# Order of the units and of the table loads in the long convolutions of an encoder layer

## The chip, the core and the metric

The kernel runs on one core of one Trainium2 chip. The metric is the device time of one execution in microseconds (us), smaller being better.

The engines are called here as the profile calls them: PE (TensorE, matrix products), PEld (its weight loads), DVE (VectorE), ACT (ScalarE), POOL (GpSimd) and SP (SyncE, which here only starts transfers).

## What is computed

One encoder layer for two sequences, of 528 and 272 tokens with their 16 meta tokens (below: the long and the short sequence): a windowed attention and a Hyena long convolution side by side, gated and merged, then a mixture of experts. The change touches only the long convolutions:

```
def _long_conv(z, kf):
    L = z.shape[1]
    zf = jnp.fft.rfft(z, n=2 * L, axis=1)
    return jnp.fft.irfft(zf * kf[None], n=2 * L, axis=1)[:, :L]

def _hyena(u, conv_w, conv_b, kf, skip):
...
    v, x1, x2 = jnp.split(uc, HY_ORDER + 1, axis=-1)
    z = v.astype(F32)
    sk = skip.astype(F32)
    for o, gate in enumerate((x1, x2)):
        z = gate.astype(F32) * (_long_conv(z, kf[:, o]) + sk[o] * z)
    return z.astype(u.dtype)
```

`kf` is the spectrum of a filter that the kernel makes itself. The 512 channels are four tiles of 128.

## The kernel before

Three stages follow one another: `stage_mix` (projections, attention, the short convolution), `stage_hyena` (the long convolutions) and the block of `stage_route` and `stage_experts`. At the end of each of the first two stands a barrier of all engines.

`stage_hyena` has eight **units**, one for each sequence and channel tile. `UNITS` (line 935) lists them as (sequence, tile): sequence 0 is the long one, 1 the short one. Each unit is gone through twice, once for each order of the recurrence `o`. Such a pass is a **turn**, and `TURNS` (line 936) fixes the 16 of them: turns 0 to 3 are `o` = 0 of units 0 to 3, turns 4 to 7 are `o` = 1 of the same units, and turns 8 to 15 are the same for units 4 to 7. A turn whose unit is long is called a long turn.

The Fourier transforms are matrix products with tables: `ahead` (to the spectrum) and `back` (from it), one set for each length, each with a small `_rest` table for the last rows. Values are split in a high and a low part, and a product is three PE passes (lines 250 to 252) over them. The steps of a turn:

- `hgen` (PE, lines 1266 and 1267): filter taps from the features and the output weights, three tiles. It needs both halves of the weights of its channel tile `j`, with the wait `pe.wait_ge(w_lo, j + 1)`. These halves are made once per channel tile by `wsum` (POOL, lines 315 and 316), `whi` (ACT, lines 1369 and 1370) and `wlo` (DVE, line 1459).
- `decay` (DVE, line 1483): taps times a decay table that SP loads (three buffers); for a long turn `hsum` (POOL, lines 1115 and 1116) adds and subtracts them; `hhi` (ACT, lines 1383 to 1388) and `hlo` (DVE, lines 1492 and 1494) split them.
- `kf` (PE, lines 250 to 252 and 1282) makes the filter's spectrum with `ahead`. It needs all three `hlo` of its turn. A long turn has two `kf` steps of 14 products, a short one has one. `kfout` (ACT, lines 1399 and 1400) takes it out of PSUM.
- `fold` (POOL, lines 1130 and 1131, long turns of `o` = 0 only), `zt` (PE transposes, lines 1302 to 1308), `zhi` (ACT, lines 1411 to 1414), `zlo` (DVE, lines 1501 and 1502), `fwd` (PE, again 14 products a step, two steps in a long turn).
- `mul` (DVE, line 1515), `comb` (POOL, lines 1144 and 1145), `yt` (PE transposes, line 1336), `yhi` (ACT), `ylo` (DVE), `inv` (PE, with `back`), `gate` (DVE) and, in long turns, `unfold` (POOL).

`hyena_steps` (line 943) gives each step a place, its turn's number plus the constant of `PLACE` (line 937), and sorts all steps by it. Every engine goes through this one list in its order and takes its own steps. So the steps of neighbouring turns overlap, and an engine that waits holds back whatever stands behind on it. The products go round robin through four pairs of PSUM banks.

The tables of `stage_hyena` are loaded by POOL's queue, from within that list at `wsum` of tile 0 and of tile 1 (lines 1100 to 1107). Tile 0's sums were made in the stage before. Decay tables and rows of the sequences come by SP's queue. In turns 0 to 3 before: short tile 0, long tile 0, long tile 1, short tile 1.

Of the kernel before, what the change touches and what calls it, by code (L numbers as in the profile page):

```python
# [310 lines left out]
def sum_weights(nc, g, j):  # L311

    both = g.wraw[:, :, j * P:(j + 1) * P].rearrange("k (r o) c -> k r o c", r=2)
    dst = g.wsum[:, :, :].rearrange("k (r o) c -> k r o c", r=2)
    nc.gpsimd.tensor_tensor(dst[:, 0, :, :], both[:, 0, :, :], both[:, 1, :, :], ALU.add)
    nc.gpsimd.tensor_tensor(dst[:, 1, :, :], both[:, 0, :, :], both[:, 1, :, :], ALU.subtract).then_inc(g.w_sum, 1)
# [615 lines left out]


WRAW_AT = 217984 + 64
UNITS = [(1, 0), (0, 0), (0, 1), (1, 1), (0, 2), (0, 3), (1, 2), (1, 3)]
TURNS = [(4 * g + k, o) for g in range(2) for o in range(2) for k in range(4)]
PLACE = {"wsum": -3.2, "whi": -3.35, "wlo": -2.65, "hgen": -2.95, "decay": -2.65, "hsum": -2.35, "hhi": -2.25, "hlo": -1.55, "kf": -1.05, "kfout": -0.95,
         "fold": -0.95, "zt": -0.9, "zhi": -0.85, "zlo": -0.5, "fwd": -0.25, "mul": 0.1, "comb": 0.35, "yt": 0.65, "yhi": 0.75, "ylo": 1.05, "inv": 1.5, "gate": 1.75, "unfold": 2.55}
# [4 lines left out]
def hyena_steps():  # L943
# [7 lines left out]
    for i, (u, o) in enumerate(TURNS):  # L951
        s = UNITS[u][0]
        for k in ("hgen", "decay", "hhi", "hlo") + (("hsum",) if s == 0 else ()):
# [10 lines left out]
def stage_hyena(g):  # L964
    nc, io, S = g.nc, g.io, g.sem
# [6 lines left out]
    back = [sb(f"back{s}", [P, 2, BT[s], BN[s]], F32R) for s in range(2)]  # L972
    back_rest = [sb(f"back{s}_rest", [96, PAIRS[s], BN[s]], F32R) for s in range(2)]
# [34 lines left out]
    ahead_in, back_in = S("hy_ahead0 hy_ahead1"), S("hy_back0 hy_back1")  # L1008
# [6 lines left out]
    def length(u):  # L1015
        return UNITS[u][0]
    parts = [PAIRS[length(u)] for u, o in TURNS]
# [4 lines left out]
    place = {i: same[s].index(i) for s in same for i in same[s]}  # L1022
    which = {u: UNITS[u][1] for u in range(len(UNITS))}

# [4 lines left out]
    def earlier(u):  # L1029

        return UNITS.index((length(u), which[u] - 2))

# [51 lines left out]
    with nc.Block() as block:  # L1084
        @block.gpsimd
        def _(pool):
            def table_load(tab, dst, sem):
                nc.gpsimd.dma_start(dst[:, :, :, :], io[tab].rearrange("x (t p) w -> p x t w", p=P)).then_inc(sem, 16)
# [5 lines left out]
            for st in steps:  # L1094
                if st[0] == "wsum":
                    j = st[1]
                    if j:
                        pool.wait_ge(w_lo, j)
                        sum_weights(nc, g, j)
                    if j == 0:  # L1100
                        table_load("ahead0", ahead[0], ahead_in[0])
                        nc.gpsimd.dma_start(ahead_rest[0][:, :], io["ahead0_rest"]).then_inc(ahead_in[0], 16)
                    if j == 1:
                        table_load("back1", back[1], back_in[1])
                        nc.gpsimd.dma_start(back_rest[1][:, 0, :], io["back1_rest"]).then_inc(back_in[1], 16)
                        table_load("back0", back[0], back_in[0])
                        nc.gpsimd.dma_start(back_rest[0][:, :, :], io["back0_rest"].rearrange("b p w -> p b w")).then_inc(back_in[0], 16)
                elif st[0] == "hsum":
# [59 lines left out]
        def _(sp):  # L1168
            rows = g.hyS.rearrange("(q j p) t -> j p q t", q=3, p=P)

            def decay_in(i):
                s, j = UNITS[TURNS[i][0]]
                d = decay[i % 3]
                if i >= 3:
                    sp.wait_ge(decayed, MT * (i - 2))
                c = slice(j * P, (j + 1) * P)
                if s == 0:
                    for r in range(2):
                        sp.dma_start(d[:, r, 0:2, :], io["decay0"][r, 0:2 * P, c].rearrange("(t p) c -> p t c", p=P)).then_inc(dec_in[i % 3], 16)
                    sp.dma_start(d[0:REST[0], :, 2, :], io["decay0"][:, 2 * P:FOLD, c].rearrange("r p c -> p r c")).then_inc(dec_in[i % 3], 16)  # L1180
                else:
                    sp.dma_start(d[:, 0, 0:2, :], io["decay1"][0:2 * P, c].rearrange("(t p) c -> p t c", p=P)).then_inc(dec_in[i % 3], 16)
                    sp.dma_start(d[0:REST[1], 0, 2, :], io["decay1"][2 * P:LENS[1], c]).then_inc(dec_in[i % 3], 16)

            def vx_load(u):
                s, j = UNITS[u]
                at = (0, LENS[0] + 1)[s]
                if j >= 2 and s:
                    sp.wait_ge(gate_mul, turn_of(earlier(u), 0) + 1)
                if j >= 2 and s == 0:  # L1190
                    sp.wait_ge(folded, 2 * folds_before[turn_of(earlier(u), 0)] + 2)
                sp.dma_start(vx[s][j % 2][:, :, 0:LENS[s]], rows[j, :, 0:2, at:at + LENS[s]]).then_inc(vx_in[buf(u)], 16)
# [1330 lines left out]
```

## Time and profile before

| | before |
|---|---|
| Median of 3 runs | 1928.94 us (1928.61 to 1931.06) |
| Profiled execution, span | 1928.8 us |
| PE busy | 1835.1 us (95%) |
| DVE busy | 1417.5 us (73%) |
| ACT busy | 1197.9 us (62%) |
| POOL busy | 312.4 us (16%) |
| Mean granted PE clock | 0.976 of full |

The span runs from the first to the last instruction of one profiled execution. It is 0.1 us from the median of the timed runs; no other time of the profiled execution is given. Busy times are those of the whole span. The long convolutions take its part from about 417 to 609 us. The granted clock is told as a share of full speed, 1.0 being 2.4 GHz and 0.5 being 1.2 GHz.

### The profile page before, as it was taken

Reading aid. Unit: us, or ns where it says so; the run is one execution under the profiler, and the core shown is the slowest. Engines: PE = TensorE matmul, PEld = TensorE weight load, DVE = VectorE, ACT = ScalarE, POOL = GpSimd, SP = SyncE. Lnnn points to the kernel's source line nnn. Section 1 sums busy time; section 2 is a strip of 40 time slices with the busy share of each in tenths; the row PEclk is TensorE's granted clock in tenths of the full one; section 3 lists DMA queues with packets and bytes.
Section 4 is the critical chain, followed back from the end, with each engine's and each line's share of the span. In section 5 each row is a group of like instructions: output and inputs, shape, how many; then the busy total and the mean of one; then the engine's idle time right before and its main releaser. Section 6 shows DMA issues by size and latency. Waiting matters only on the chain.

```text
span 1928.8 us, 25301 instructions
## 1 busy us (share of the span) xinstructions
PE 1835.1 (95%) x9358; PEld 1447.1 (75%) x9358; DVE 1417.5 (73%) x1451; ACT 1197.9 (62%) x1332; POOL 312.4 (16%) x220
## 2 busy tenths in 40 slices
PE   5999999978998999599999999999999999999996
PEld 4989877868998988477777777777777777777774
DVE  4673321138885533699999999999999999999996
ACT  4225666644554311377777777777777777777775
POOL 1223211225653500001001000000000110010010
PEclk8999999988999999799999999999999999999998
DMA  6333222145115662599999999999999999999994
GB/s 188 99 82 102 72 71 77 41 140 162 33 44 177 220 230 109 200 356 357 385 385 373 380 382 379 374 391 371 373 382 387 376 379 379 375 376 390 379 352 175
DMA packets 240329, 506.53 MB, mean 263 GB/s; under 512 B 22017, under 2 KB 56681, under 8 KB 240200
## 3 DMA queue, kind: packets, MB, share of 16 engines
q1 hardware_dynamic: 229640, 484.64, 69.6%
q0 software_dynamic: 10624, 21.03, 4.4%
q8 instruction: 40, 0.66, 0.1%
q14 instruction: 25, 0.20, 0.0%
HBM read 474.64 MB, written 31.28 MB: 262 GB/s over the span
## 4 chain that ended last, share of the span: by engine, by line
PE 65%; DVE 2%; ACT 1%; issue 0%; DMA 0%; POOL 0%; DVEq 0%; POOLq 0%; ACTq 0%
PE bank L251 21%; PE bank L250 21%; PE bank L252 21%; PE bank L2141 2%; PE bank L1938 1%; PE bank L1924 0%; DMA gathered<-ffn_rows,slot_tokens 0%; PE bank L245 0%; DVE top_values L1844 0%; DVE top_index L1846 0%; ACT we_hi L2199 0%; DVE affinity L1847 0%; DVE gated L1785 0%; DVE we_lo L2273 0%; DVE bank L1786 0%
## 5 line engine op out<-in xcount | busy, mean ns | idle before, releaser
L2273 DVE TENSOR_TENSOR we_lo<-w_ring,we_hi 128x2048 fp32r<-128x2048 f32 x382 | 864.9, 2288 | 71.1 <-ACT we_hi L2199 64.9
L2199 ACT ACTIVATE we_hi<-w_ring 128x2048 fp32r<-128x2048 f32 x380 | 724.3, 1914 | 98.1 <-PE bank L252 98.0
L250 PE MATMUL bank<-we_hi,gathered_turned_hi 128*100 128x512 f32 x1024 | 404.3, 395 | 1.5 <-DVE gathered_turned_lo L2277 1.5
L251 PE MATMUL bank<-we_lo,gathered_turned_hi 128*100 128x512 f32 x1024 | 404.3, 395 | 0.0
L252 PE MATMUL bank<-we_hi,gathered_turned_lo 128*100 128x512 f32 x1024 | 401.4, 392 | 0.0
L250 PEld LDWEIGHTS bank<-we_hi,gathered_turned_hi 128*100 128x100 f32 x1024 | 168.7, 165 | 67.8 <-issue 1.7
L252 PEld LDWEIGHTS bank<-we_hi,gathered_turned_lo 128*100 128x100 f32 x1024 | 168.7, 165 | 67.0
L251 PEld LDWEIGHTS bank<-we_lo,gathered_turned_hi 128*100 128x100 f32 x1024 | 168.4, 164 | 64.0
L250 PE MATMUL bank<-normed_hi,w_hi 128*128 128x400 f32 x544 | 197.7, 363 | 10.1 <-ACT u_padded L657 5.1
L250 PE MATMUL bank<-we_hi,hidden_turned_hi 128*100 128x512 f32 x512 | 204.4, 399 | 0.0
L251 PE MATMUL bank<-we_lo,hidden_turned_hi 128*100 128x512 f32 x512 | 202.2, 395 | 0.0
L252 PE MATMUL bank<-we_hi,hidden_turned_lo 128*100 128x512 f32 x512 | 201.7, 394 | 0.0
L251 PE MATMUL bank<-normed_lo,w_hi 128*128 128x400 f32 x544 | 188.5, 347 | 0.0
L252 PE MATMUL bank<-normed_hi,w_lo 128*128 128x400 f32 x544 | 188.0, 346 | 0.0
L2119 POOL DMA_INDIRECT residual_rows<-expert_out,slots_now x15 | 42.1, 2807 | 840.2 <-DVE expert_out L2307 840.2
L250 PEld LDWEIGHTS bank<-normed_hi,w_hi 128*128 128x128 f32 x544 | 103.3, 190 | 31.7 <-issue 18.2
L913 POOL TENSOR_TENSOR w_lo<-w_raw,w_hi 128x2048 fp32r<-128x2048 f32 x17 | 79.1, 4652 | 277.3 <-ACT w_hi L622 277.3
L252 PEld LDWEIGHTS bank<-we_hi,hidden_turned_lo 128*100 128x100 f32 x512 | 84.3, 165 | 34.4
L250 PEld LDWEIGHTS bank<-we_hi,hidden_turned_hi 128*100 128x100 f32 x512 | 84.6, 165 | 31.8
L251 PEld LDWEIGHTS bank<-we_lo,hidden_turned_hi 128*100 128x100 f32 x512 | 84.4, 165 | 31.2
L251 PEld LDWEIGHTS bank<-normed_lo,w_hi 128*128 128x128 f32 x544 | 103.3, 190 | 0.0
L252 PEld LDWEIGHTS bank<-normed_hi,w_lo 128*128 128x128 f32 x544 | 103.2, 190 | 0.1
(318 smaller groups left out, 2586.8 us busy)
## 6 DMA issues: line engine op xcount, KB each, us to landing
w_ring<-in_w_exp_gate SPq DMA_DIRECT2D x64, 2048.0 KB, 14.2
w_ring<-in_w_exp_up SPq DMA_DIRECT2D x64, 2048.0 KB, 13.7
w_ring<-in_w_exp_down SPq DMA_DIRECT2D x64, 2048.0 KB, 15.3
w_raw<-in_w_in SPq DMA_DIRECT2D x68, 256.0 KB, 4.2
gate_rows<-gate_sig SPq DMA_DIRECT2D x16, 400.0 KB, 2.5
sig_pair<-gate_rows SPq DMA_DIRECT2D x8, 800.0 KB, 6.1
hy_conv_rows<-u_conv SPq DMA_DIRECT2D x12, 400.5 KB, 3.3
w_out<-in_w_out SPq DMA_DIRECT2D x8, 512.0 KB, 8.5
```

The costliest lines, as they stand in the source:

```text
L250: nc.tensor.matmul(out, whi, xhi, start=first, stop=False)
L251: nc.tensor.matmul(out, whi, xlo, start=False, stop=False)
L252: return nc.tensor.matmul(out, wlo, xhi, start=False, stop=last)
L913: nc.gpsimd.tensor_tensor(wlo[c % 2][:, :, :], raw[c % 3][:, :, :], whi[c % 2][:, :, :].bitcast(F32), ALU.subtract).then_inc(w_lo, 1)
L1938: last = nc.tensor.matmul(g.ps[6][0:m, 0:E], hT[:, k, 0:m], wrg[:, k, :], start=(k == 0), stop=(k == KT - 1))
L2119: pool.indirect_dma_start(g.accS[:, :], bass.IndirectOffsetOnAxis(ap=cur[0:SLOTS, 0:1], axis=0), ye[0:SLOTS, :], None, compute_op=ALU.add) ...
L2141: last = nc.tensor.transpose(tb[n % 2][:, k * P:k * P + SLOTS], src, ident[0:SLOTS, 0:SLOTS])
L2199: act.activation(whi[(2 * k + half) % 4][:, :], ring[k % RING][:, half * HC:(half + 1) * HC], ACT.Copy).then_inc(w_hi, 1)
L2273: nc.vector.tensor_tensor(wlo[u][:, :], ring[k % RING][:, half * HC:(half + 1) * HC], whi[u][:, :].bitcast(F32), ALU.subtract).then_inc(w_ ...
```

## The change

Two things are put in another order, and nothing is added or left out. In `UNITS` the second short unit (1, 1) goes from the fourth place to the second, so turns 0 to 3 become short tile 0, short tile 1, long tile 0, long tile 1. Turns 4 to 7 follow with it; units 4 to 7 are as they were. And the load of the short `back` tables goes from `wsum` of tile 1 to `wsum` of tile 0, ahead of the long `ahead` tables.

```
-UNITS = [(1, 0), (0, 0), (0, 1), (1, 1), (0, 2), (0, 3), (1, 2), (1, 3)]
+UNITS = [(1, 0), (1, 1), (0, 0), (0, 1), (0, 2), (0, 3), (1, 2), (1, 3)]
...
                     if j == 0:
+                        table_load("back1", back[1], back_in[1])
+                        nc.gpsimd.dma_start(back_rest[1][:, 0, :], io["back1_rest"]).then_inc(back_in[1], 16)
                         table_load("ahead0", ahead[0], ahead_in[0])
                         nc.gpsimd.dma_start(ahead_rest[0][:, :], io["ahead0_rest"]).then_inc(ahead_in[0], 16)
                     if j == 1:
-                        table_load("back1", back[1], back_in[1])
-                        nc.gpsimd.dma_start(back_rest[1][:, 0, :], io["back1_rest"]).then_inc(back_in[1], 16)
                         table_load("back0", back[0], back_in[0])
```

What stands in a row on POOL at the start of `stage_hyena`. The names end in numbers of their tensors: `ahead_94` and `back_98` are the short tables, `ahead_93` and `back_97` the long ones; `wout_sum_diff` is written by `wsum`.

```order
 L1088 DMA ahead_94_3774<-in_ahead 128x4x548
 L1091 DMA ahead_rest_3776<-in_ahead_rest 96x548
+L1088 DMA back_98_3778<-in_back 128x8x272
+L1102 DMA back_rest_3780<-in_back_rest 96x272
 L1088 DMA ahead_93_3773<-in_ahead 128x4x1064
-L1102 DMA ahead_rest_3775<-in_ahead_rest 96x1064
-L315 TENSOR_TENSOR wout_sum_diff_56<-filt_wout_55 64x256
-L316 TENSOR_TENSOR wout_sum_diff_56<-filt_wout_55 64x256
-L1088 DMA back_98_3778<-in_back 128x8x272
-L1105 DMA back_rest_3780<-in_back_rest 96x272
+L1104 DMA ahead_rest_3775<-in_ahead_rest 96x1064
```

Two DMA starts now stand ahead of the first `wsum` (lines 315 and 316) of this stage, which was behind four such starts and is behind six.

On DVE, from the last `hlo` of turn 0 to the first `hlo` of turn 1. `taps_ahead_back` is the target of a long turn's `decay`, `taps_sum_diff` that of a short one's; L1459 is `wlo`.

```order
 L1494 TENSOR_TENSOR taps_rest_3810<-taps_sum_diff_3804,taps_rest_3810 16x256
 L1459 TENSOR_TENSOR wout_lo_3795<-wout_sum_diff_56,wout_hi_twice_3794 64x512
-L1483 TENSOR_TENSOR taps_ahead_back_3800<-bank,decay_3798 128x512
-L1483 TENSOR_TENSOR taps_ahead_back_3801<-bank,decay_3798 128x512
-L1483 TENSOR_TENSOR taps_ahead_back_3800<-bank,decay_3798 9x512
+L1483 TENSOR_TENSOR taps_sum_diff_3805<-bank,decay_3798 128x256
+L1483 TENSOR_TENSOR taps_sum_diff_3802<-bank,decay_3798 128x256
+L1483 TENSOR_TENSOR taps_sum_diff_3803<-bank,decay_3798 16x256
 L1459 TENSOR_TENSOR wout_lo_3795<-wout_sum_diff_56,wout_hi_twice_3794 64x512
-L1483 TENSOR_TENSOR taps_ahead_back_3801<-bank,decay_3799 128x512
-L1492 TENSOR_TENSOR taps_lo_3809<-taps_sum_diff_3805,taps_hi_3808 128x512
+L1483 TENSOR_TENSOR taps_ahead_back_3800<-bank,decay_3799 128x512
```

The kinds of steps keep their order here; those of turn 1 are half as wide, and their result is no longer added and subtracted by POOL.

## Rows read from the trace of the kernel before

**Rows 1.** Stretches: length, busy us of PE, PEld, DVE, ACT, POOL, PE clock, DMA share, GB/s.

```profile
421.20:428.10 6.90, 6.16 (x26) 5.03 (x27) 5.89 (x15) 2.81 (x6) 4.91 (x7) 0.52 1.16 369
430.90:437.40 6.50, 0.85 (x7) 0.38 (x5) 3.28 (x6) 4.69 (x11) 4.14 (x6) 0.79 1.21 334
437.40:448.60 11.20, 8.83 (x39) 8.37 (x40) 11.14 (x7) 3.25 (x7) 11.13 (x16) 0.51 1.39 342
452.70:594.00 141.30, 141.30 (x1153) 138.84 (x1152) 114.31 (x197) 73.71 (x178) 73.71 (x100) 1.00 0.15 45
```

**Rows 2.** Who PE waited for from 414 to 612 us: total, times, longest.

```profile
PE bank L250 <- DVE z_turned_rest L1502: 2.9, 1, 2.9
PE bank L250 <- DVE taps_rest L1494: 2.8, 2, 2.4
PE bank L1266 <- ACT spectra L1400: 2.8, 1, 2.8
```

**Rows 3.** PE in order of time: start us, us, line, operation, xcount, [idle before].

```profile
421.16 0.55 PE L1266 MATMUL bank<-wout_hi_twice,features_hi_lo 128*128 128x256 f32 x1 [6.47 <-DVE wout_lo L1459]
422.58 0.41 PE L1266 MATMUL bank<-wout_hi_twice,features_hi_lo 128*128 128x256 f32 x1
426.42 0.60 PE L250 MATMUL bank<-ahead,taps_hi 128*128 128x274 f32 x1 [0.44 <-DVE taps_rest L1494]
437.35 0.57 PE L250 MATMUL bank<-ahead,z_turned_hi 128*128 128x274 f32 x1 [2.87 <-DVE z_turned_rest L1502]
443.25 0.59 PE L250 MATMUL bank<-ahead,taps_hi 128*128 128x266 f32 x1 [2.37 <-DVE taps_rest L1494]
452.63 0.37 PE L250 MATMUL bank<-ahead,z_turned_hi 128*128 128x266 f32 x1
456.16 0.29 PE L250 MATMUL bank<-ahead,taps_hi 128*128 128x266 f32 x1
457.89 0.29 PE L1266 MATMUL bank<-wout_hi_twice,features_hi_lo 128*128 128x256 f32 x1
458.14 0.60 PE L1306 MATMUL bank<-ident,v_x_folded 128*128 128x128 f32 x4
458.71 0.37 PE L250 MATMUL bank<-ahead,taps_hi 128*128 128x266 f32 x1
```

**Rows 4.** POOL in order of time: the starts of two transfers, `wsum` of tile 1.

```profile
421.10 0.72 POOL L315 TENSOR_TENSOR wout_sum_diff<-filt_wout 64x256 f32<-64x256 f32 x1 [0.47 <-DVE wout_lo L1459]
422.46 0.94 POOL L1088 DMA_DIRECT2D back<-in_back  x1
423.40 0.56 POOL L1105 DMA_DIRECT2D back_rest<-in_back_rest  x1
```

**Rows 5.** DVE in order of time: `wlo` of tile 1, then steps of turns 0 to 3.

```profile
426.40 0.69 DVE L1459 TENSOR_TENSOR wout_lo<-wout_sum_diff,wout_hi_twice 64x512 fp32r<-64x512 f32 x1
435.33 0.69 DVE L1483 TENSOR_TENSOR taps_ahead_back<-bank,decay 128x512 f32<-128x512 f32 x1 [2.17 <-DMA decay<-in_decay]
437.89 4.00 DVE L1492 TENSOR_TENSOR taps_lo<-taps_sum_diff,taps_hi 128x512 fp32r<-128x512 f32 x1
444.51 5.29 DVE L1459 TENSOR_TENSOR wout_lo<-wout_sum_diff,wout_hi_twice 64x512 fp32r<-64x512 f32 x1
450.28 0.68 DVE L1492 TENSOR_TENSOR taps_lo<-taps_sum_diff,taps_hi 128x512 fp32r<-128x512 f32 x1
458.78 0.77 DVE L1492 TENSOR_TENSOR taps_lo<-taps_sum_diff,taps_hi 128x256 fp32r<-128x256 f32 x1
524.05 1.07 DVE L1492 TENSOR_TENSOR taps_lo<-taps_sum_diff,taps_hi 128x512 fp32r<-128x512 f32 x1
```

**Rows 6.** POOL's last operations of the two runs beside the long DVE rows.

```profile
441.31 1.19 POOL L1131 TENSOR_TENSOR v_x_folded<-v_x 128x265 f32<-128x265 f32 x1
449.22 1.19 POOL L1131 TENSOR_TENSOR v_x_folded<-v_x 128x265 f32<-128x265 f32 x1
```

**Rows 7.** ACT: `kfout` of turn 0.

```profile
432.95 0.47 ACT L1399 ACTIVATE spectra<-bank,conv_taps 128x274 f32<-128x274 f32 x1
```

## The prediction

> **What bounds the kernel now.** I read the stretches first. From 452.7 to 594 us PE is busy without a gap at full clock [rows 1], so nothing that only reorders other engines' work can shorten that part. The loss is in the fill of the pipeline before it. Over 421.2 to 428.1 and 437.4 to 448.6 the clock is near 0.5, which is 1.2 GHz; PE had stood idle before the first of these and nearly idle (0.85 of 6.5 us) before the second [rows 1]. The waits name who held PE back there: `zlo` of turn 0, the `hlo` steps and `kfout`, that is, mostly the chain through DVE [rows 2]. In order of time PE starts the stage at 421.16, `fwd` of turn 0 at 437.35 after 2.87 idle, `kf` of turn 1 at 443.25 after 2.37 idle, and `kf` of turn 2 at 456.16 [rows 3]. From there on it never waits until the stage's tail. That last moment is my yardstick.
>
> DVE itself was held up. At 435.33 it had waited 2.17 for the decay table of turn 2, and two operations that take 0.68 when undisturbed lasted 4.00 and 5.29 [rows 5]. Both read two operands from SBUF, both lay beside an unbroken run of POOL operations, and both were over shortly before the run's last operation ended, itself stretched to 1.19 [rows 6]. So POOL held DVE for 3.3 and 4.6 us.
>
> **The yardstick.** Up to `kf` of turn 2, PE now has less to do, since turn 1 is short and not long. A `kf` or `fwd` step of a long turn takes 457.89 - 456.16 = 1.73, so `kf` of a long turn 3.46; its `fwd` took 456.16 - 452.63 = 3.53 [rows 3]. Short ones have one step, 14 products of 274 columns in place of 266, so 1.73 x 274/266 = 1.8. The transposes take 458.71 - 458.14 = 0.57 in a long turn [rows 3] and I estimate 0.3 for half as many. The `hgen` steps of turns 1 and 3 swap their sizes and both lie before the mark. Work that goes behind the mark: 1.66 + 1.73 + 0.27 = 3.66 us. PE's whole work is the same, so the change breaks even if `kf` of turn 2 starts at 456.16 - 3.66 = **452.5** at full clock. Earlier is gain, later is loss.
>
> **The change part by part.**
>
> *Two transfer starts ahead of `wsum`.* They cost POOL 0.94 + 0.56 [rows 4]. POOL had idled 0.47 before `wsum` of tile 1 [rows 4], so it comes 1.0 us later. ACT's `whi` and DVE's `wlo` follow it: `wlo` of tile 1 goes from 426.40 [rows 5] to 427.4 and ends at 428.0.
>
> *`hgen` of turn 1 has channel tile 1 now.* It went on at 422.58 without a wait [rows 3], with tile 0. It now waits for that `wlo`, to 428.05. Behind it on PE stands `kf` of turn 0, which goes from 426.42 [rows 3] to 429.4, after six products at 0.21. PE has idled over five microseconds, so I take 1.2 GHz for it: 14 products at 274/1.2 ns are 3.2 us, end 432.6. The cover for this delay is ACT: it took `kf` out at 432.95 only [rows 7], since POOL and ACT were late with other steps. It now can at 432.7. So this wait of three microseconds costs almost nothing.
>
> *The decay table of turn 2.* Those of turns 0 and 1 stand before it on SP's queue, and turn 1's is now half as large. The 2.17 of waiting [rows 5] goes. What is late next is `hgen` of turn 2, done at 433.5. DVE begins there at 433.6 instead of 435.33.
>
> *The chain on DVE from there to the last `hlo` of turn 2.* Six long `decay` at 0.65, three short `hlo` at 0.41 and two long ones at 0.65, `zlo` twice 0.7, `mul` 1.4, `wlo` 0.65: 10.0 us. Waits on other engines: 0.3 for `zhi`, 0.2 for `hgen` of turn 3. `hlo` tile 1 of turn 1 meets POOL's run of `hsum`, `wsum`, `hsum`; that run must stop for DVE's next `decay`, so the wait is at most about 1.9. `hlo` tile 0 of turn 2 meets `comb` and `hsum`, at most 1.15. I take both whole, since the long DVE rows ended like that. Then the last `hlo` of turn 2 is asked for at 433.6 + 10.0 + 0.5 + 3.05 = 447.2. On the way `fwd` of turn 0 starts at 435.7 and `kf` of turn 1 at 439.7, both earlier than before (437.35 and 443.25).
>
> *The last `hlo` of turn 2.* It was at no engine's edge; now `kf` of turn 2 starts when it ends. POOL is then in a run of `hsum`, `fold`, `hsum`, `fold` that waits for nobody and goes on to 452.1. The wait lies between 0 (the row at 450.28) and 4.6 (at 444.51) [rows 5]. I take 3.3, that of the row of the same line at the same place in the program, 437.89. It ends at 447.2 + 3.3 + 0.65 = **451.2**, which is 1.3 before break-even.
>
> By the Trainium skill (SBUF — State Buffer, "Who interferes with whom"), whichever of a DVE operation with two SBUF inputs and a POOL operation starts first has the shared port for that one instruction. By it the wait would be at most one POOL operation of 0.72, and the sum 2.6 us lower. The row at 524.05 (0.39 over) agrees with that, those at 437.89 and 444.51 do not.
>
> *The clock.* Between `fwd` of turn 1, 445.2 to 447, and 451.2 PE stands idle for four microseconds, as it did before 437.35. So `kf` of turn 2 begins at 1.2 GHz. Before, full clock came back after 443.25 to 448.6, 5.3 us of unbroken work, or after 421.2 to 428.1, 6.9 us [rows 1, 3]. Half of it is lost: 2.7 to 3.4. I take 2.7. Lower bound 0, if the gap is short.
>
> *The order of the tables.* It costs nothing beyond the two starts. Every table is loaded by the time that the same bytes had landed before, and no PE row waited for a table [rows 2]. The long `ahead` is wanted only from 451, where before it was wanted at 443.25.
>
> *From turn 2 on.* Turns 2 to 7 are now long, long, short, short, long, long, exactly like turns 8 to 13, which run in the gapless part [rows 1]. New is only that turns 6 to 9 are four long ones in a row. PE has no slack there, DVE is at 114.31 of 141.30 [rows 1]: nothing. The tail is the same.
>
> **Sum.** -1.3 + 2.7 = +1.4 us on the span of 1928.8, so 1930.2. The span lies 0.1 under the median of the runs: **1930.3 us**. A measurement of this kernel can tell about 0.2%, 3.9 us, from no change, so this is no change.
>
> **Rivals.** *DVE is served soon (faster).* If POOL gives way after one operation each time (0.4, as at 524.05), the three waits are 1.2 in place of 6.35, and `kf` of turn 2 starts at 446.0, 6.5 before break-even. The gaps on PE are then short; with half the clock price, 1.35, the sum is -5.1: 1923.8. For it: from 458 us on the waits are all small, 0.1 to 0.4 at 458.78 and 524.05 [rows 5]. Against it: both long ones fell in the fill. Chance 0.25.
>
> *The long turn 3 is late (slower).* Its decay table is now long and stands behind both long sequence loads on SP's queue. If it lands 2.2 late, as turn 2's did [rows 5], the whole DVE chain behind it moves by 2.2; and with 6.9 us at 1.2 GHz in place of 5.3 the clock costs 0.7 more. The sum is 1.4 + 2.9 = +4.3: 1933.2. It decides if `kf` of turn 2 starts after about 453.0. Against it: up to that table the same bytes are queued as before, and it is wanted at 442. Chance 0.28.
>
> *The tables' order is the gain and it is hidden anyway*: that falls in the forecast, within a microsecond.
>
> **Chances.** Forecast 0.47. Its own range goes from a last wait of 0 (1.4 - 3.3 = -1.9) to one of 4.6 with 3.4 for the clock (1.4 + 1.3 + 0.7 = +3.4): 1927 to 1932.3. Faster by over 0.2% 0.25, within 0.2% 0.47, slower 0.28. The range to hold the time 8 times in 10 takes in both rivals' values and leaves out their far ends: 1923.5 to 1934.5.
>
> **What would show it.** Right: one PE wait of over 5 us for `wlo` (line 1459) just after the first `hgen`; no DVE wait for a decay table in turn 2; `kf` of turn 1 near 440; a DVE row of lines 1492 or 1494 lasting over 2 us before `kf` of turn 2, and that at about 451 with the clock at 0.5. Wrong: `kf` of turn 2 before 448 or after 453.5, PE idle anywhere between 460 and 590, or a PE wait for a transfer.

## The result, and the profile after

| | before | after |
|---|---|---|
| Median of the runs made side by side (5 and 5) | 1928.69 us (1927.15 to 1931.06) | 1937.31 us (1932.18 to 1937.66) |
| Profiled execution: its own time, span | span 1928.8 us | 1937.62 us, span 1935.8 us |
| PE busy | 1835.1 us | 1834.7 us |
| DVE busy | 1417.5 us | 1416.7 us |
| ACT busy | 1197.9 us | 1198.1 us |
| POOL busy | 312.4 us | 314.8 us |
| Mean granted PE clock | 0.976 | 0.976 |

The change made the kernel slower: the ratio is 1.0039, 95% interval [1.0028, 1.005], where I had forecast 1930.3 us and no change. 1937.31 lies outside my range of 1923.5 to 1934.5. Wherever both are on record, an execution's time is 1.7 to 1.9 above its span. So the profiled execution of before took some 1930.6 (an estimate), above its median, and the two spans differ by 7.0 where the medians differ by 8.6.

The engines' work is what it was, so the time is in waits. This is who PE waited for from 414 to 612 us after the change, in the columns of [rows 2]:

```profile
PE bank L1266 <- DVE wout_lo L1459: 11.9, 2, 6.5
PE bank L1266 <- DVE taps_ahead_back L1483: 6.4, 1, 6.4
...
PE bank L1336 <- DVE taps_ahead_back L1483: 2.4, 1, 2.4
PE bank L250 <- DVE taps_rest L1494: 1.7, 1, 1.7
PE bank L250 <- DVE gated_parts L1558: 1.0, 2, 0.8
```

Two of the lines are new and stand outside the fill. In order of time, PE after the change, in the columns of [rows 3]:

```profile
421.06 0.55 PE L1266 MATMUL bank<-wout_hi_twice,features_hi_lo 128*128 128x256 f32 x1 [6.47 <-DVE wout_lo L1459]
428.13 0.55 PE L1266 MATMUL bank<-wout_hi_twice,features_hi_lo 128*128 128x256 f32 x1 [5.45 <-DVE wout_lo L1459]
434.69 0.37 PE L250 MATMUL bank<-ahead,z_turned_hi 128*128 128x274 f32 x1 [0.82 <-issue]
438.46 0.40 PE L250 MATMUL bank<-ahead,taps_hi 128*128 128x274 f32 x1 [1.75 <-DVE taps_rest L1494]
444.70 1.08 PE L1336 MATMUL bank<-ident,y_spectrum 128*128 128x128 f32 x4 [2.44 <-DVE taps_ahead_back L1483]
448.98 0.39 PE L250 MATMUL bank<-ahead,taps_hi 128*128 128x266 f32 x1
522.98 0.36 PE L250 MATMUL bank<-ahead,z_turned_hi 128*128 128x266 f32 x1 [0.80 <-DVE gated_parts L1558]
536.04 0.36 PE L250 MATMUL bank<-ahead,z_turned_hi 128*128 128x266 f32 x1 [0.23 <-DVE gated_parts L1558]
552.37 0.37 PE L1266 MATMUL bank<-wout_hi_twice,features_hi_lo 128*9 128x256 f32 x1 [6.36 <-DVE taps_ahead_back L1483]
```

**The fill became better, by more than the forecast had it.** `kf` of turn 2 starts at 448.98, where the forecast had 451.2 (and the fast rival 446.0). Break-even was 452.5, so 3.5 us are gained (3.4, counted from the stage's first `hgen`, 421.06 now and 421.16 in [rows 3]).

**Everything was lost behind it.** The stretches of after, in the columns of [rows 1]:

```profile
448.96:517.20 68.24, 68.22 (x557) 67.01 (x558) 59.04 (x94) 36.50 (x86) 49.91 (x66) 1.00 0.23 63
517.20:541.00 23.80, 22.69 (x184) 21.87 (x183) 19.95 (x31) 9.98 (x23) 6.75 (x11) 1.00 0.03 12
541.00:552.00 11.00, 5.01 (x42) 4.77 (x40) 0.61 (x2) 2.41 (x7) 2.68 (x5) 0.93 0.50 148
552.00:557.40 5.40, 5.03 (x22) 4.07 (x23) 5.29 (x11) 2.00 (x4) 4.31 (x6) 0.52 0.15 42
557.40:597.00 39.60, 39.60 (x324) 38.99 (x323) 31.52 (x56) 20.98 (x52) 16.66 (x23) 1.00 0.01 3
```

From 541 to 552 PE works 5.01 of 11.00 us and DVE 0.61. Then PE works 5.03 us at a granted clock of 0.52, about 1.2 GHz, which at 2.4 GHz would have taken some 2.4 less. DVE says what it stood waiting for; here is its row, and under it SP's queue in order of time (SPq, the same columns; the length of an SP row takes in its waits):

```profile
551.53 0.69 DVE L1483 TENSOR_TENSOR taps_ahead_back<-bank,decay 128x512 f32<-128x512 f32 x1 [10.39 <-DMA decay<-in_decay]
```

```profile
531.00 13.14 SPq L1208 DMA_DIRECT2D mixer_rows<-x_long  x2
544.19 2.53 SPq L1199 DMA_DIRECT2D x_long<-hy_conv_rows  x2
546.78 0.90 SPq L1199 DMA_DIRECT2D x_short<-hy_conv_rows  x2
547.72 0.95 SPq L1179 DMA_DIRECT2D decay<-in_decay  x2
```

The decay table of turn 12 was started at 547.72 only. SP goes through its queue in order: the store of unit 3 (line 1208), then four loads of the next `x2` rows (line 1199), then that table (line 1179). The store waits until unit 3 is finished, and the second `x_long` load waits until that store has landed (the pair took SP 2.53 us, 0.94 in the kernel before). A long unit is finished by `unfold` of its second turn, here turn 7, on POOL:

```profile
542.52 0.66 POOL L1159 TENSOR_TENSOR x_long<-gated_parts 128x265 f32<-128x265 f32 x1
543.12 0.66 POOL L1160 TENSOR_TENSOR x_long<-gated_parts 128x263 f32<-128x263 f32 x1
```

In the kernel before unit 3 was the short one, stored right after its `gate`. This is the same queue in the kernel before, and the first use of that table on DVE there:

```profile
537.45 0.34 SPq L1208 DMA_DIRECT2D mixer_rows<-x_short  x1
537.83 0.94 SPq L1199 DMA_DIRECT2D x_long<-hy_conv_rows  x2
538.82 0.90 SPq L1199 DMA_DIRECT2D x_short<-hy_conv_rows  x2
539.76 0.95 SPq L1179 DMA_DIRECT2D decay<-in_decay  x2
```

```profile
544.07 0.69 DVE L1483 TENSOR_TENSOR taps_ahead_back<-bank,decay 128x512 f32<-128x512 f32 x1 [0.67 <-PE bank L1267]
```

From issue (539.76) to need (544.07) there were 4.3 us. In after issue to use took 551.53 - 547.72 = 3.8. So the old order had about half a microsecond of slack there (1.1 by the 3.2 us that the same load took in the half-dose run below), and nothing in a list of PE's waits showed it.

**The account.** I measure the stage from its first `hgen` to PE's first product of the next stage: 609.04 - 421.16 = 187.9 before, 616.38 - 421.06 = 195.3 after, +7.4. Fill -3.4; waits 6.36 + 0.80 + 0.23 = +7.4; low clock behind the long wait +2.4; that makes +6.4. Of the other 1.1, some 0.4 lie in the tail: from the last wait on "issue" to the end PE took 4.97 us (611.41 to 616.38) where it took 4.59 before (604.45 to 609.04), at a granted clock of 0.54 in place of 0.60. The rest is not traced to a row. The repaired kernel below, which has no long wait, has 0.5 too much by the same sum, so a part of it is probably that 3.66 was too low for the work that moved behind the mark.

### The profile page after: what moved, and what is told of

The parts are those of the page before. It is cut to its first block, busy times and chain, and to the rows that moved or that the text cites. A ratio compares the mean times of both kernels' runs of the same rounds, so it can differ in the third digit from the quotient of the medians.

```text
span 1935.8 us, 25302 instructions
## 1 busy us (share of the span) xinstructions
PE 1834.7 (95%) x9358; PEld 1446.9 (75%) x9358; DVE 1416.7 (73%) x1451; ACT 1198.1 (62%) x1332; POOL 314.8 (16%) x220
## 4 chain that ended last, share of the span: by engine, by line
PE 65%; DVE 2%; ACT 1%; issue 0%; POOL 0%; DVEq 0%; POOLq 0%; ACTq 0%
PE bank L251 21%; PE bank L250 21%; PE bank L252 20%; PE bank L2141 2%; PE bank L245 1%; PE bank L1938 1%; PE bank L1924 0%; DVE top_values L1844 0%; DVE top_index L1846 0%; ACT we_hi L2199 0%; DVE affinity L1847 0%; DVE gated L1785 0%; DVE we_lo L2273 0%; POOL out L2133 0%; DVE bank L1786 0%
```

## The experiments

Each was timed in rounds beside the kernel before on the same chip. "Stage" is the length as defined above, from the one profiled execution; what lies outside it varies by 5.2 us from profile to profile (1735.7 to 1740.9; the first `hgen` starts anywhere from 418.6 to 421.7), so the stage tells small things better than the span. Inside the stage the fill varies too: from the first `hgen` to `kf` of turn 2 it is 35.0 in before and 34.3 in e2, 27.7 in e1 and 27.1 in e5, pairs whose edits lie behind the fill. A difference there of under 0.8 is therefore not told from nothing by one profile each. The ratio is to the kernel before in the same rounds, where its median was 1927.37 to 1928.22. In the kernels with the old order of units (before, e2, e4, e10, e11) `kf` of turn 2 has 3.66 us more of work ahead of it.

| run | median us | ratio to before [95%] | stage us | `kf` of turn 2 |
|---|---|---|---|---|
| before | 1928.69 | | 187.9 | 456.16 |
| after | 1937.31 | 1.0039 [1.0028, 1.005] | 195.3 | 448.98 |
| e1_decay12_first | 1926.49 | 0.9991 [0.9983, 1.0] | 186.6 | 448.10 |
| e2_before_decay12_first | 1929.04 | 1.0001 [0.9993, 1.001] | 187.1 | 455.52 |
| e3_units_only | 1936.25 | 1.0038 [1.0025, 1.0052] | 195.0 | 449.05 |
| e4_tables_only | 1927.96 | 0.9995 [0.9986, 1.0003] | 186.8 | 454.85 |
| e5_pool_break | 1926.27 | 0.9991 [0.9981, 1.0] | 184.8 | 447.89 |
| e6_decay12_half | 1929.84 | 1.0012 [1.0003, 1.0021] | 191.6 | 447.93 |
| e7_wsum_first | 1927.82 | 0.9994 [0.9985, 1.0002] | 184.8 | 447.91 |
| e8_second_group_alternates | 1926.66 | 0.9992 [0.9983, 1.0] | 186.8 | 447.97 |
| e9_long_back_late | 1926.6 | 0.9994 [0.9985, 1.0003] | 184.0 | 448.10 |
| e10_before_long_back_late | 1930.12 | 1.0013 [1.0004, 1.0022] | 190.7 | 459.55 |
| e11_before_pool_breaks | 1930.08 | 1.0009 [1.0, 1.0018] | 188.7 | 455.72 |
| e12_decay3_first | 1922.77 | 0.9972 [0.9962, 0.9983] | 184.3 | 444.86 |

### The table of turn 12 ahead of the store that waits

```
             for u in range(4):
                 store_out(u)
-                if u < 2:
+                if u < 3:
                     decay_in(10 + u)
             for u in range(4, 8):
                 x2_load(u)
-            for i in range(12, 16):
+            for i in range(13, 16):
                 decay_in(i)
```

In the changed kernel:

> The changed kernel with one edit: SP starts the decay table of turn 12 before it waits to store the fourth unit. Theory A (the loss sits in SP's queue: the table of turn 12 stands behind the store of unit 3, now a long unit that is stored after turn 7's unfold): the 10.4 us wait of DVE near 541 and the 6.4 us gap of PE near 546 go, with 2.5 us of half clock behind it; 1927 to 1929.5, at or a little below the kernel before. Rival B (four long turns in a row overload DVE and POOL, and the decay table would only have been waited for by an engine that is late anyway): the gap near 546 shrinks but the time stays within 2 us of the change, about 1935. Rival C (the fill is what lost): no change, 1937.

And the same edit in the kernel before:

> The same edit in the kernel before. Theory A: DVE did not wait for that table there, so 1928.7 within 1 us. If it gains more than 2 us, the edit has a worth of its own and the first kernel's gain can't be put down to the change.

In the changed kernel the edit takes back all of the loss and a little more: 1926.49 in place of 1937.31. Of these 10.8 us the stage gives 8.7; the other 2 lie outside it, within the scatter told above. The table is started at 530.48, while the store still goes out at 543.08; DVE finds it there at 541.23 and waits for PE instead:

```profile
530.48 1.17 SPq L1179 DMA_DIRECT2D decay<-in_decay  x2
543.08 0.34 SPq L1208 DMA_DIRECT2D mixer_rows<-x_long  x1
```

```profile
541.23 0.69 DVE L1483 TENSOR_TENSOR taps_ahead_back<-bank,decay 128x512 f32<-128x512 f32 x1 [0.99 <-PE bank L1267]
```

In the kernel before the same edit does nothing (1.0001). So it is no general improvement; it mends what the new order of the units broke.

### Each part of the change alone

In the kernel before, the line of `UNITS` alone, with the tables where they were:

> The order of units alone, tables as before. Theory A: the long wait comes from the units' order, so 1935 to 1938 as the change, perhaps 0.5 to 1 us less since the wsum of tile 1 is 1.5 us earlier. Rival D (the order of the tables costs the time): 1929 or less.

In the changed kernel the old `UNITS`, so that the order of the tables alone is new:

> The order of the tables alone. Theory A: 1928.7 within 1.5 us; wsum of tile 1 comes 1 us later, and turn 1 with tile 0 does not wait for it. Rival D: 1935 or more.

The order of the units alone gives the whole result, 1.0038, with the same rows:

```profile
531.05 13.17 SPq L1208 DMA_DIRECT2D mixer_rows<-x_long  x2
547.43 0.95 SPq L1179 DMA_DIRECT2D decay<-in_decay  x2
```

```profile
551.33 0.69 DVE L1483 TENSOR_TENSOR taps_ahead_back<-bank,decay 128x512 f32<-128x512 f32 x1 [10.11 <-DMA decay<-in_decay]
```

Its `kf` of turn 2 starts at 449.05, so the gain in the fill comes from the units too. The order of the tables alone cannot be told from nothing (0.9995 [0.9986, 1.0003]).

The two runs differ in one thing that I had put down to the units. DVE's first step of turn 2, with the units alone and then with the tables alone:

```profile
434.28 0.69 DVE L1483 TENSOR_TENSOR taps_ahead_back<-bank,decay 128x512 f32<-128x512 f32 x1 [3.74 <-DMA decay<-in_decay]
```

```profile
433.88 0.67 DVE L1483 TENSOR_TENSOR taps_ahead_back<-bank,decay 128x512 f32<-128x512 f32 x1
```

With the units alone DVE waits 3.74 us for the decay table of turn 2, longer than the 2.17 of the kernel before. With the tables alone it does not wait for it at all. The other runs agree: all five profiles with the old order of the tables (before, e2, e3, e10, e11) show this wait, 1.45 to 3.74 us, and none of the nine with the new order does. So it is the order of the tables on POOL's queue that let this table of SP's queue land in time. `kf` of turn 2 comes 27.9 us after the first `hgen` either way, in after and with the units alone.

### Half of the dose

In the changed kernel the table behind the store, but ahead of the four loads:

```
             for u in range(4):
                 store_out(u)
                 if u < 2:
                     decay_in(10 + u)
+            decay_in(12)
             for u in range(4, 8):
                 x2_load(u)
-            for i in range(12, 16):
+            for i in range(13, 16):
                 decay_in(i)
```

> The changed kernel with turn 12's decay table behind unit 3's store but ahead of the four loads of x2 that stood between them on SP's queue. In the changed kernel the store was issued at 544.19 less its own issue, the loads took SP from 544.19 to 547.72, and the table's issue began at 547.72. Theory A (the queue's order makes the loss, microsecond for microsecond): the table is issued 3.5 us earlier, at about 544.2, DVE's wait of 10.39 falls to about 6.9, PE's wait of 6.36 to about 2.9, and the time falls from 1937.3 by 3.5 for the wait and by 0 to 2.5 for the clock, to 1931.3 to 1933.8. Rival (the loss comes from something else that the full repair also removed, such as traffic): the wait does not follow the issue time.

```profile
543.15 1.38 SPq L1179 DMA_DIRECT2D decay<-in_decay  x2
```

```profile
546.37 0.69 DVE L1484 TENSOR_TENSOR taps_ahead_back<-bank,decay 128x512 f32<-128x512 f32 x1 [6.26 <-DMA decay<-in_decay]
```

The wait follows the issue: started 4.6 us earlier (3.5 against `kf` of turn 2), the table is waited for 4.1 less, 6.26 in place of 10.39, and PE stands idle 2.24 in place of 6.36. The time, 1929.84, is lower than I had said (1931.3 to 1933.8): in the stage the edit gives back 3.7 of the 8.7, as its rows say, and the rest of the 7.5 us between the medians lies outside the stage. Of the stage's 191.6 - 186.6 = 5.0 over the full repair, 2.24 + 0.34 + 0.39 are waits of PE that the repair does not have and 0.35 is a longer one in the tail. The rest is the clock: in a stretch around it PE's mean granted clock was 0.91 over 19 us, which is up to 1.7:

```profile
541.00:560.00 19.00, 16.03 (x118) 14.86 (x116) 12.24 (x21) 7.63 (x19) 11.62 (x16) 0.91 0.34 103
```

### A pause of POOL lets DVE in

With the repair PE still had a wait of 0.8 at 522, behind a DVE step of 4.31 us beside an unbroken run of POOL. In the repaired kernel:

```
                     pool.wait_ge(vx_in[buf(u)], landed(u))
+                    if (i, k) == (9, 0):
+                        pool.wait_ge(h_lo, MT * 9 + 1)
```

> The kernel with turn 12's decay table ahead of unit 3's store, and in it one wait more: ahead of the first `fold` of turn 9 POOL waits until DVE has done the `hlo` step of tile 0 of turn 9. Without that wait this step (line 1492) began at 514.31 and lasted 4.31 us, to 518.62, while POOL ran without a pause to 518.06; the folds of turn 9 began at 515.19. Theory C (DVE is held as long as POOL's operations follow each other without a gap): with the gap the step ends within about 0.7 us of the end of POOL's `comb` at 515.2, so it lasts 1.5 to 1.7 us, PE's wait of 0.8 for `gated_parts` (line 1558) goes, and the span falls by 0.8 to 1.0. Rival D (the step's length has another cause, and POOL's run only happens to lie beside it): the step still lasts about 4.3, POOL stands idle for it, and PE's gap stays or grows. The time itself should be 1926.5 less about 1, which is inside the noise; the rows decide.

DVE's step with the repair alone, and then with the pause:

```profile
514.31 4.31 DVE L1492 TENSOR_TENSOR taps_lo<-taps_sum_diff,taps_hi 128x512 fp32r<-128x512 f32 x1
```

```profile
514.13 1.47 DVE L1494 TENSOR_TENSOR taps_lo<-taps_sum_diff,taps_hi 128x512 fp32r<-128x512 f32 x1
```

Here are POOL's operations around the pause, in which DVE's step ends:

```profile
514.39 0.65 POOL L1147 TENSOR_TENSOR y_spectrum<-zk_imag,zk_real 128x264 f32<-128x264 f32 x1
515.73 0.76 POOL L1132 TENSOR_TENSOR v_x_folded<-v_x 128x265 f32<-128x265 f32 x1 [0.68 <-issue]
```

Theory C holds: forecast were 1.5 to 1.7, and PE's wait of 0.80 falls to 0.23. The stage is 1.8 shorter, of which 0.7 lies in the fill, where nothing was changed. In the timed runs 1926.27 and 1926.49 can't be told apart.

The same POOL work spread by another order of the second group, in the repaired kernel without the pause:

```
-UNITS = [(1, 0), (1, 1), (0, 0), (0, 1), (0, 2), (0, 3), (1, 2), (1, 3)]
+UNITS = [(1, 0), (1, 1), (0, 0), (0, 1), (0, 2), (1, 2), (0, 3), (1, 3)]
```

> The kernel with turn 12's decay table ahead of unit 3's store, and the second group's units in the order long, short, long, short in place of long, long, short, short, so that turns 6 to 9 are no longer four long ones in a row (6, 7, 8 long, 9 short). Theory C2 (four long turns in a row make POOL's unbroken run of `hsum`, `fold` and `comb` of 508 to 518): no DVE step over 2.5 us between 505 and 525, and PE's 0.8 goes, 1 us less. Rival: the alternation needs a decay table or a load in another order than SP's queue gives, or the tail, which now ends long, short, has a longer wait for the last long turn; then the time is the same or up to 4 us more. Time 1925 to 1930.

No DVE step near 514 is held any more and the 0.8 is gone, as theory C2 says. In its place PE waits 4.46 in the tail where it was 2.04, the rival's half. The stage is 186.8 against 186.6: a gain turned into a longer tail.

### Pauses of POOL in the fill of the kernel before

This tests the premise of my sum, that POOL's hold of DVE is what the fill loses by.

```
                         pool.wait_ge(w_lo, j)
+                        if j == 3:
+                            pool.wait_ge(h_lo, MT + 2)
...
                     pool.wait_ge(f_mul, n + 1)
+                    if i == 0 and q == 0:
+                        pool.wait_ge(w_lo, 4)
```

> The kernel before, with two pauses of POOL in the fill: ahead of `wsum` of channel tile 3 it waits until DVE has done `hlo` tile 1 of turn 1 (the row at 437.89 that lasted 4.00), and ahead of `comb` of turn 0 until DVE has done `wlo` of tile 3 (the row at 444.51 that lasted 5.29). Theory C, on which my prediction's whole sum rests (the gap of POOL lets DVE in): the first lasts about 0.7, the second 1.3 to 2.0, `kf` of turn 1 starts near 440.5 instead of 443.25, `kf` of turn 2 at 452 to 454 instead of 456.16, and the time falls by 2 to 4 us, to about 1925. Rival D: the rows keep their length, POOL loses what it waits, and the time rises by up to 4. Rival E (the holds are there, but PE's fill hangs on something else): the rows become short and `kf` of turn 2 stays within 0.5 of 456.16.

The two rows named did become short, 4.00 to 0.68 and 5.29 to 1.94. But in each run of POOL the next such step was held in their place:

```profile
437.15 0.68 DVE L1496 TENSOR_TENSOR taps_lo<-taps_sum_diff,taps_hi 128x512 fp32r<-128x512 f32 x1
...
438.46 3.55 DVE L1498 TENSOR_TENSOR taps_rest<-taps_sum_diff,taps_rest 9x512 fp32r<-9x512 f32 x1
...
443.32 1.94 DVE L1463 TENSOR_TENSOR wout_lo<-wout_sum_diff,wout_hi_twice 64x512 fp32r<-64x512 f32 x1
...
445.74 4.77 DVE L1496 TENSOR_TENSOR taps_lo<-taps_sum_diff,taps_hi 128x512 fp32r<-128x512 f32 x1
```

The first went with a pause of POOL of 0.82. For the second POOL did not even have to stop: DVE was let in during the `fold` at 444.68, itself stretched to 1.19. `kf` of turn 1 came at 442.06 (443.25 before), where theory C had 440.5. `kf` of turn 2 moved by 0.44 (455.72 for 456.16) but, counted from the first `hgen` of each, not at all (35.1 and 35.0), and the time did not fall (1.0009 [1.0, 1.0018]). This is rival E by its numbers, but not by its cause: the holds were moved, not removed. What the fill would be without any hold stays open.

### `wsum` ahead of the long tables' starts

In the kernel with the pause:

```
-                    if j:
+                    if j > 1:
                         pool.wait_ge(w_lo, j)
                         sum_weights(nc, g, j)
                     if j == 0:
                         table_load("back1", back[1], back_in[1])
                         nc.gpsimd.dma_start(back_rest[1][:, 0, :], io["back1_rest"]).then_inc(back_in[1], 16)
+                        pool.wait_ge(w_lo, 1)
+                        sum_weights(nc, g, 1)
```

> The kernel of the POOL pause with, besides, `wsum` of channel tile 1 issued on POOL right after the first long-back... short-back table, so ahead of the two transfer starts of the long ahead table. My prediction put two starts ahead of `wsum` at 1.0 us on `wlo` of tile 1 and at nothing on PE. If the start of `wlo` (line 1459, tile 1) hangs on `wsum`, it comes up to 1.4 us earlier (from 426.59 in the kernel that has only the table moved), PE's wait for it falls by as much, and `kf` of turn 2 comes up to 1 us earlier. If ACT's order is what holds `wlo` (its steps for the taps stand ahead of `whi`), nothing moves. Time 1924.5 to 1926.5; the rows decide.

PE's wait for `wlo` of tile 1 falls from 5.45 to 4.44, so it did hang on `wsum`, and `kf` of turn 1 comes 1.1 earlier (437.48 for 438.55). `kf` of turn 2 does not move, 447.91 for 447.89. The reason stands on DVE, a wait for the decay table of turn 3:

```profile
442.79 0.69 DVE L1487 TENSOR_TENSOR taps_ahead_back<-bank,decay 128x512 f32<-128x512 f32 x1 [3.11 <-DMA decay<-in_decay]
```

That is the wait that my slow rival named. In the profile of after the same wait is 3.19, to 443.86. What DVE gained ahead of it was spent there. It is not in every run with this order on SP's queue: in e1, e6 and e8 the table was there by 442.66 to 442.74, when PE's `hgen` let DVE begin, and in e5 the wait was 0.21, to 442.77.

### What makes the table of turn 3 late

Its start (424.70 in the kernel above) can't come earlier, since it waits for turn 0's buffer, but it took 18 us to land. First the long back table out of its way, in the kernel just described and in the kernel before (where the short back table stays under `if j == 1`, and the line `if j == 3` is added between the two):

```
-                    if j == 1:
+                    if j == 3:
                         table_load("back0", back[0], back_in[0])
```

> The kernel with turn 12's table moved, POOL's pause and `wsum` first, and in it the long back table (two transfers on POOL) started behind the `wsum` of channel tile 3, at about 436 instead of 422. In the kernel without this, DVE waited 3.11 us for the decay table of turn 3 to 442.79, although its transfer had been started at about 424.5, and PE waited 2.35 for DVE; the DMA engines were busy all that time (share 1.1 to 1.3 from 420 to 444). Theory T (the table of turn 3 is late because other transfers share the DMA engines with it): it lands at least 2 us earlier, DVE begins its decay step when `hgen` of turn 3 is done, PE's 2.35 goes, and `kf` of turn 2 starts 1 to 2 us earlier than 447.91; the time is 1922 to 1925. Rival S (the table is late for another reason, such as a fixed latency or its own start): the wait stays above 2.5 us and nothing moves. The back table itself is wanted at about 470.

> The kernel before, with only the long back table started behind the `wsum` of channel tile 3. There DVE waited 2.17 us for the decay table of turn 2, to 435.33. By theory T that wait falls to under 1 us and the chain behind it moves as much; POOL's hold of DVE in the fill stays, with the same edges, so that `kf` of turn 2 comes 0 to 2 us earlier than 456.16. Time 1926 to 1929. By rival S nothing moves.

Theory T falls for this table and this transfer. The table is first used at 442.80 where it was 442.79, with DVE's wait for it now 0.33 because DVE itself was held 2.55 just before; against the first `hgen` it came 0.6 earlier, not 2. In the kernel before the wait for turn 2's table goes from 2.17 to 1.90 only, and the kernel became slower, with POOL's starts and sums moved against DVE's steps (a hold of 5.17 at 438.14, and a new one of 3.29 at 443.94 on the last `hlo` of turn 1, for which PE waited 6.14; by its ratio, 1.0013, it is within what a measurement can tell, and the stage is 2.8 longer). That transfers of the two queues do touch each other is shown by another pair of runs: the order of the short back and long ahead tables decided whether DVE waited for the table of turn 2 (above).

Then the table ahead of the two long sequence loads on its own queue, in the kernel with `wsum` first:

```
-            for i in range(1, 4):
+            vx_load(TURNS[1][0])
+            decay_in(3)
+            for i in range(2, 4):
                 vx_load(TURNS[i][0])
-            for i in range(3, 7):
+            for i in range(4, 7):
                 decay_in(i)
```

> The kernel with turn 12's table moved, POOL's pause and `wsum` first, and on SP's queue the decay table of turn 3 ahead of the two long sequence loads (of turns 2 and 3) in place of behind them. The table can't be issued before about 424.7, when DVE is done with turn 0's; the long loads, issued at 421.42 there, come about 5 us later. Moving the back table left the table's landing at 442.8. Theory Q (the transfers that were started ahead of it on the same queue hold it, my slow rival's mechanism): it lands 3 us or more earlier, DVE's wait of 3.11 goes and the step at 442.79 comes at 440 to 441, when `hgen` of turn 3 is done; PE's 2.35 falls below 1; `kf` of turn 2 at 446 to 447.5 in place of 447.91, unless the `fold` of turn 2 now waits for its sequence. Time 1924 to 1926. Rival S: it still lands at 442 to 443, and nothing moves or the fold is late, up to 2 us more.

SP's queue and DVE in this kernel:

```profile
422.47 0.91 SPq L1183 DMA_DIRECT2D decay<-in_decay  x2
423.86 0.90 SPq L1196 DMA_DIRECT2D v_x<-hy_conv_rows  x2
```

```profile
439.75 0.69 DVE L1489 TENSOR_TENSOR taps_ahead_back<-bank,decay 128x512 f32<-128x512 f32 x1 [1.97 <-PE bank L1273]
```

The rows agree with theory Q but do not prove it. DVE no longer waits for the table but for PE's `hgen`, as soon as that is done. How much earlier the table landed is not shown: the whole stage began 2.24 earlier here, and counted from the first `hgen` the table was started at 3.9 us in both kernels and was there by 21.2 at the latest, where it was 22.0. From start to use that is at most 17.3 us here and 18.1 there, but 17.1 in e5, with the long loads still ahead of it. What held DVE now was PE, which ran `kf` of turn 1 at half clock (in the kernel that this one was made from the clock was 1.00 there). In the columns of [rows 1]:

```profile
435.50:439.00 3.50, 3.43 (x15) 3.43 (x16) 2.24 (x5) 0.50 (x1) 2.90 (x4) 0.52 1.21 301
```

PE's wait of 2.35 is 0.38 now. Against its own first `hgen` (418.56), `kf` of turn 2 comes 26.3 us after it, where it was 27.1. That is 0.8, hardly more than fills differ by without an edit, and the stage is 184.3 in place of 184.8. Yet the runs are 1922.77, 5 us below the kernel that it was made from, and at 0.9972 [0.9962, 0.9983] the only version that is faster than the kernel before beyond what a measurement tells (0.2%). Of its 8.6 us of span against the kernel before (1920.2 for 1928.8) the stage gives 187.9 - 184.3 = 3.6. Another 2.6 lie ahead of it, where the first `hgen` came at 418.56 and not 421.16, and 2.4 behind it. I have found nothing in this edit that reaches the stages around, and have no cause for those 5.0 us. The half-dose kernel's profile is 5.2 shorter than before outside the stage as well (1735.7 for 1740.9), with an edit that can't reach those stages either. So the 0.9972 is not shown to be the worth of this edit.

## Why the prediction was wrong, point by point

- **The step that failed** is the one headed *From turn 2 on*: "Turns 2 to 7 are now long, long, short, short, long, long, exactly like turns 8 to 13, which run in the gapless part [rows 1]. [...] nothing." The comparison was of the kinds of turns, on engines. It left out SP's queue, in which the store of unit 3 stands ahead of the table of turn 12, and no queue of the second group has such a store ahead of a table (their stores come last). Unit 3 became long, so its store waits for `unfold` of turn 7. That is a wait of 10.39 us on DVE, which costs 6.36 of PE and 2.4 of clock, 8.8 in all; the repair shortens the stage by 195.3 - 186.6 = 8.7. Moving one transfer gives it back and more; half the move gives back 3.7 of the 8.7. This is shown.
- *DVE is at 114.31 of 141.30*, in the same step, was also no proof of slack. In the four long turns in a row POOL had an unbroken run, DVE was held 4.29 us at 515.24, and PE waited 0.80 and 0.23. The pause of POOL brings the first down to 0.23. I had named "PE idle anywhere between 460 and 590" as a sign of being wrong, and it was the sign, above all with the 6.36 at 552.
- *`hgen` of turn 1 waits for `wlo`.* Right in place and size: 5.45 us to 428.13, forecast 428.05, and it cost nothing that I can see, since `fwd` of turn 0 came at 434.69 (forecast 435.7) and `kf` of turn 1 at 438.46 (439.7). That the two starts ahead of `wsum` are worth 1.0 us on `wlo` is shown, as is that this 1.0 did not reach `kf` of turn 2.
- *The decay table of turn 2.* Right by luck. That wait is gone, and DVE began turn 2 at 432.71 (433.6). But I had put it down to turn 1's table being half as large, and with the units alone, where that is so too, the wait was 3.74. The order of the tables took it away, of which I had said that it costs and brings nothing.
- *The chain on DVE.* The last `hlo` of turn 2 was asked for at about 447.7, forecast 447.2. This is right by errors that cancel. Turn 3's table was waited for 3.19, where I had 0.2 for `hgen` there (in the repaired kernel `hgen` alone cost 1.59). Against that DVE had begun 0.9 sooner, and the second hold that I had put at 1.15 did not come. The first hold was 1.7 over, where I had at most 1.9.
- *The last `hlo` of turn 2.* Mis-sized. I took a hold of 3.3; the row says 0.5, and my lower bound of 0 was the nearer end:

```profile
447.72 1.21 DVE L1494 TENSOR_TENSOR taps_rest<-taps_sum_diff,taps_rest 9x512 fp32r<-9x512 f32 x1
...
448.95 0.69 DVE L1523 TENSOR_TENSOR y_turned_lo<-bank,y_turned_hi 128x512 fp32r<-128x512 f32 x1
```

  So `kf` of turn 2 came at 448.98 and not 451.2, 2.2 better.
- *The clock.* Mis-sized for the same reason. Without the long hold PE had no long gap there. The clock was low from 444.7 to 448.2, ahead of `kf` of turn 2, and full from then on:

```profile
444.70:448.20 3.50, 3.50 (x16) 3.12 (x16) 3.42 (x7) 1.64 (x4) 3.34 (x4) 0.53 1.56 371
448.20:449.00 0.80, 0.70 (x7) 0.48 (x5) 0.77 (x2) 0.59 (x1) 0.80 (x2) 1.00 1.56 223
```

  The 2.7 that I added behind the mark were 0. With the 2.2 that makes the 4.9 between my +1.4 for the fill and the -3.4 measured. The rival *DVE is served soon* was thus nearer to the fill than my forecast.
- *The order of the tables costs nothing.* Right for the time, shown by the run with it alone (0.9995), though it moved the table of turn 2, as said above.
- *The slow rival* had the wait right, 3.19 for the table of turn 3 where I had 2.2. That the two long sequence loads ahead of it are the cause is likely, but not shown (above). It had the price wrong: the kernel with the repair did not have this wait, and its `kf` of turn 2 came only 0.2 sooner after the first `hgen` (27.7 for 27.9); taking it away in the last experiment brought 0.8. The time came near what it gave (1933.2) only by way of another transfer.
- *The port of DVE and POOL.* By the Trainium skill (SBUF — State Buffer, "Who interferes with whom") the engine whose operation starts first has the shared port for that one instruction. The rows bear it out in part: the last `hlo` of turn 2 and the step of 1.47 were served after one POOL operation, while those of 4.31 and 4.77 lay beside five or more, one behind the other. In the repaired kernel POOL began a new operation at 514.57, 515.19, 515.90, 516.61 and 517.32 while DVE stood at the one it had asked for at 514.31.

## What to carry to other kernels

Before moving a piece of work, go through every in-order queue that names it, the transfer queue above all: a transfer that waits for the end of one piece holds up all that stands behind it, and a longer piece in that place can starve an engine a hundred microseconds later. For such a transfer ask how long before its need it is started, not whether anyone waits for it today; here it was 4.3 us, for a load that took 3.8 from start to use (3.2 in the half-dose run). A gain in the fill is only seen when the rest of the pipeline can keep it, so compare lengths of the stage between fixed marks as well as the whole time.

## What I had not expected of the hardware

A DVE operation with two SBUF inputs can be passed over again and again by a run of POOL operations (4.31 us for a step of 0.68), or be let in after the first (1.2 to 1.5 us). The two pauses that POOL made (0.68 and 0.82 us) let it in. If the run goes on afterwards, the next such operation can be the one that is held (3.55 and 4.77 us). What decides between the two I could not find out.

A table of 128 KB parts that was started at 424.70 was used only at 442.79, with two long sequence loads started 3.3 us ahead of it on its queue. With those behind it, it was there by 439.75 at the latest, started at 422.47: 18.1 us and at most 17.3. Taking a table of 2128 KB on POOL's queue out of the same time moved its first use by 0.01 us, and by 0.6 counted from the first `hgen`. But another order of two tables on POOL's queue took away the wait for the decay table of turn 2 on SP's (1.45 to 3.74 us in five profiles, none in nine).
